# Folding a four-column projection into a padded weight tile, splitting the next weights ahead of a block's end, and joining two groups of gate matmuls

## The reference, cut to what matters

```python
def even_mixer(xn, w_in, w_out, k_ln_g, k_ln_b, rel_bias, rope_h, rope_i):
    qa, ka, va, qi, ki, wi, qb, kb, vb = _split(xn @ w_in, EVEN_SPLITS)   # qi 256, ki 64, wi 4 columns
    ...
    qi = apply_rope(qi.reshape(bsz, seq, IDX_HEADS, IDX_DIM), *rope_i)
    ki = apply_rope(layer_norm(ki, k_ln_g, k_ln_b), *rope_i)
    ya = dsa_sparse_attention(qa, ka, heads(va, A_HEADS), qi, ki, wi)
# inside dsa_sparse_attention, for each block of 128 queries:
    rel = jax.nn.relu(jnp.einsum('bqhd,bsd->bqhs', qib, k_idx))
    score = jnp.einsum('bqhs,bqh->bqs', rel, wib)
    _, idx = lax.top_k(score, topk)
def odd_mixer(xn, w_in, w_out, forget_b, sinks, rope_h):
    qc, kc, vc, fc, qd, kd, vd = _split(xn @ w_in, ODD_SPLITS)            # fc: 8 columns, the forget gate
    log_f = jax.nn.log_sigmoid(fc.astype(jnp.float32) + forget_b)
```

## Time and profile before

| | before |
|---|---|
| median of 3 runs | 1774.5 us (1773.67 to 1775.55) |
| time of the profiled execution | 1774.48 us |
| its span, first to last instruction | 1772.6 us |
| PE busy | 1748.9 us |
| DVE busy | 1075.9 us |
| ACT busy | 931.1 us |
| POOL busy | 614.6 us |
| mean granted TensorE clock | 0.998 |

### The profile page before, as it was taken

The page is one execution under the profiler, slowest core; times in us unless marked ns, Lnnn a source line. Parts: engine busy times, 40 slices in busy tenths (PEclk is TensorE's granted clock), DMA queues, the critical chain, the costliest instruction groups (busy, mean ns, idle before and its releaser), DMA issues.

```text
span 1772.6 us, 24077 instructions
## 1 busy us (share of the span) xinstructions
PE 1748.9 (99%) x8417; PEld 1417.4 (80%) x8417; DVE 1075.9 (61%) x1982; ACT 931.1 (53%) x1597; POOL 614.6 (35%) x342
## 2 busy tenths in 40 slices
PE   8999998999999999999999999999999999999998
PEld 5888777888888777778888888887778888888887
DVE  5777658999998799755455553224345655555113
ACT  6676565888886455554444443224565544444221
POOL 2333134211111322323444444444431444444442
PEclk9999999999999999999999999999999999999999
DMA  8422347999996222332233223334421333333332
GB/s 312 146 80 72 110 177 269 378 394 386 383 379 259 86 72 85 97 91 84 87 101 98 95 96 98 96 97 139 130 72 37 107 95 97 100 101 93 98 98 69
DMA packets 71623, 259.86 MB, mean 147 GB/s; under 512 B 13659, under 2 KB 18907, under 8 KB 59112
## 3 DMA queue, kind: packets, MB, share of 16 engines
q1 hardware_dynamic: 66744, 250.76, 41.4%
q0 software_dynamic: 4784, 7.85, 1.2%
HBM read 248.10 MB, written 18.43 MB: 150 GB/s over the span
## 4 chain that ended last, share of the span: by engine, by line
PE 60%; DVE 5%; issue 0%; POOL 0%; DMA 0%; SPq 0%; ACT 0%; DVEq 0%
PE ps L217 18%; PE ps L219 18%; PE ps L218 18%; DVE selb L1373 2%; DVE m L1372 1%; PE ps L571 1%; PE ps L610 1%; PE ps L599 1%; DVE prob L802 1%; DVE prob L817 1%; PE ps L585 0%; PE ps L618 0%; DVE selb L1350 0%; PE ps L633 0%; PE ps L361 0%
## 5 line engine op out<-in xcount | busy, mean ns | idle before, releaser
L284 POOL TENSOR_TENSOR ring_wl<-ring_w,ring_wh 128x1024 fp32r<-128x1024 f32 (+1 forms) x223 | 528.1, 2370 | 877.3 <-ACT ring_wh L276 771.1
L217 PE MATMUL ps<-two_x_high,ring_wh 128*128 128x512 f32 x1064 | 418.7, 394 | 1.1 <-DVE nmax L802 0.6
L218 PE MATMUL ps<-two_x_low,ring_wh 128*128 128x512 f32 x1064 | 414.2, 389 | 0.0
L219 PE MATMUL ps<-two_x_high,ring_wl 128*128 128x512 f32 x1064 | 414.2, 389 | 0.0
L276 ACT CAST ring_wh<-ring_w 128x1024 fp32r<-128x1024 f32 (+1 forms) x228 | 235.8, 1035 | 224.3 <-PE ps L219 214.8
L217 PEld LDWEIGHTS ps<-two_x_high,ring_wh 128*128 128x128 f32 x1064 | 199.7, 188 | 48.5 <-issue 4.2
L219 PEld LDWEIGHTS ps<-two_x_high,ring_wl 128*128 128x128 f32 x1064 | 199.7, 188 | 41.9
L218 PEld LDWEIGHTS ps<-two_x_low,ring_wh 128*128 128x128 f32 x1064 | 199.8, 188 | 41.8 <-issue 1.2
L1129 ACT ACTIVATE acc<-ps,param 128x512 f32<-128x512 f32 x88 | 68.6, 780 | 172.1 <-DVE ps L1149 172.1
L217 PE MATMUL ps<-hid_high,ring_wh 128*128 128x512 f32 (+1 forms) x374 | 141.0, 377 | 0.0
L218 PE MATMUL ps<-hid_low,ring_wh 128*128 128x512 f32 (+1 forms) x374 | 140.8, 377 | 0.0
(11 more groups left out here) (366 smaller groups left out, 3220.7 us busy)
## 6 DMA issues: line engine op xcount, KB each, us to landing
ring_w<-in_w_ff_up SPq DMA_DIRECT2D x88, 512.0 KB, 3.6
one_wg<-in_w_gate SPq DMA_DIRECT2D x32, 1024.0 KB, 7.8
one_wu<-in_w_up SPq DMA_DIRECT2D x32, 1024.0 KB, 8.1
one_wd<-in_w_down SPq DMA_DIRECT2D x32, 1024.0 KB, 8.6
ring_w<-in_w_ff_down SPq DMA_DIRECT2D x32, 448.0 KB, 3.3
ring_w<-in_w_da SPq DMA_DIRECT2D x23, 512.0 KB, 3.7
ring_w<-in_w_ff_down SPq DMA_DIRECT2D x16, 512.0 KB, 3.5
ring_w<-in_w_rel SPq DMA_DIRECT2D x12, 512.0 KB, 3.9
```

Source lines behind the costliest of these rows:

```text
L217: mm(out, wh, xh, start=start, stop=False)
L218: mm(out, wh, xl, start=False, stop=False)
L219: return mm(out, wl, xh, start=False, stop=stop)
L284: eng.tensor_tensor(self.low[s][:, 0:k, :], self.slab[s][:, 0:k, :], self.high[s][:, 0:k, :].bitcast(F32), ALU.subtract).then_inc(self.spl ...
```

## The change

1. The index weights `wi` take columns 64 to 67 of the key's tile in place of the key's second copy (60 columns of zeros follow). `tensor_weigh`, its weights' load (L1189), their scaling on POOL (L1261) and bank 3's four partial sums are gone. `wiT` comes from bank 0, and a plain copy takes the place of the reduction over four groups.
2. The key comes out on the lower half of the partitions only. SP copies it to the upper half by one DMA (`doubled`), issued ahead of the swaps, and PE waits for it before the key's mean.
3. `tensor_project` runs the three tiles interleaved for chunks 0 to 3, then tile by tile for chunks 4 to 7.
4. ACT rounds jobs 35 and 36 at the end of block one; DVE splits 35 and POOL 36 there. POOL's split of job 37 stays in block two.
5. In the odd layer all eight gate matmuls run in one go inside the first query's projection.

```diff
     def swap_halves(self, sp):
         raw, fin = self.buf["sraw"], self.buf["fin"]
+        sp.wait_ge(self.evac, 1)
+        sp.dma_start(raw[HD:P, 0, :], raw[0:HD, 0, :]).then_inc(self.doubled, 16)
         sp.wait_ge(self.evac, 3)
...
     def tensor_project(self, pe):
...
-        for j in range(DC):
+        order = [(i, j) for j in range(HALF) for i in range(3)] + [(i, j) for i in range(3) for j in range(HALF, DC)]
+        for i, j in order:
             pe.wait_ge(self.norms.xlow, j + 1)
...
-    def tensor_weigh(self, pe):
-        c, buf = self.c, self.buf
-        pe.wait_ge(self.w_ok, 1)
-        pe.wait_ge(self.norms.added, DC)
-        for j in range(DC):
-            at = 32 * (j % 4)
-            c.nc.tensor.matmul(c.ps[at:at + 4, 3, :], buf["ww"][:, j, :], c.h[:, j, :], start=(j < 4), stop=(j >= 4))\
-             .then_inc(self.weighed, 1)
...
     def tensor_after_q(self, pe):
         self.norms.columns(pe, 0)
-        pe.wait_ge(self.evac, 3)
+        pe.wait_ge(self.evac, 4)
+        pe.wait_ge(self.doubled, 16)
         nc.tensor.matmul(c.bank(1), c.k("blk64"), raw[:, 0, :], start=True, stop=True).then_inc(self.meaned, 1)
-        pe.wait_ge(self.evac, 4)
...
      def vector_evacuate(self, dve):
...
-            nc.vector.tensor_tensor(buf["sraw"][:, i, :], c.bank(i), rs[:, :], ALU.mult).then_inc(self.evac, 1)
-        dve.wait_ge(self.weighed, DC)
-        nc.vector.tensor_tensor(buf["wiT"][:, :], c.bank(3), rs[:, :], ALU.mult).then_inc(self.evac, 1)
+            rows = slice(0, P if i else HD)
+            nc.vector.tensor_tensor(buf["sraw"][rows, i, :], c.ps[rows, i, :], rs[rows, :], ALU.mult).then_inc(self.evac, 1)
+        nc.vector.tensor_tensor(buf["wiT"][:, :], c.bank(0), rs[:, :], ALU.mult).then_inc(self.evac, 1)
...
     block one, POOL:
-                select.gpsimd(pool)
+                ring.rest(pool, at["a0"] + 1)
     block one, ACT, after the chunks:
+                for i in range(2):
+                    ring.round(act, at["a0"] + i)
     block one, DVE, after the chunks:
+                ring.rest(dve, at["a0"])
     block two, POOL:
-                for i in (1, 2):
-                    ring.rest(pool, at["a0"] + i)
+                ring.rest(pool, at["a0"] + 2)
     block two, PE:
-                    gate.tensor(pe, 2, range(4, DC))
+                    gate.tensor(pe, 2, range(DC))
                     norms.mean(pe, 2)
-                select.tensor_weigh(pe)
...
-                gate.tensor(pe, 2, range(4))
     block two, ACT and DVE:
-                for i in range(2):
-                    ring.round(act, at["a0"] + i)
-                ring.rest(dve, at["a0"])
...
-        "w_idx": fm(np.concatenate([we[:, 1536:1792], ki, ki], axis=1)),
-        "w_idxw": mv(we[:, 1856:1860]),
+        "w_idx": fm(np.concatenate([we[:, 1536:1792], ki, we[:, 1856:1860], np.zeros((D, HD - 4), np.float32)], axis=1)),
```

More of the change, by code:

```diff
@@ L1170, with __init__ @@
 class Select:
-    def __init__(self, c, st, ring, j0, norms, buf):
-        self.c, self.ring, self.j0, self.norms, self.buf = c, ring, j0, norms, buf
-        self.w_in, self.w_ok, self.weighed = (st.sem(f"sel_{n}") for n in ("w_in", "w_ok", "weighed"))
+    def __init__(self, c, ring, j0, norms):
+        self.c, self.ring, self.j0, self.norms = c, ring, j0, norms
     def begin(self, st, buf):
-        self.buf.update(buf)
+        self.buf = buf
         (self.evac, self.meaned, self.step, self.sq, self.varred, self.rooted, self.rotated, self.ready, self.scored,
          self.reluded, self.accd, self.kready, self.logged, self.turned, self.taken, self.centred, self.wi_ok,
-         self.half, self.scaled, self.marked, self.swapped) = (
+         self.half, self.scaled, self.marked, self.swapped, self.doubled) = (
              st.sem(f"sel_{n}") for n in (
@@ L1185, in begin @@
                  "kready", "logged", "turned", "taken", "centred", "wi_ok", "half", "scaled", "marked",
-                 "swapped"))
-    def sync(self, sp):
-        sp.dma_start(self.buf["ww"][:, :, :], self.c.a["w_idxw"]).then_inc(self.w_in, 16)
+                 "swapped", "doubled"))
     def swap_halves(self, sp):
         raw, fin = self.buf["sraw"], self.buf["fin"]
+        sp.wait_ge(self.evac, 1)
+        sp.dma_start(raw[HD:P, 0, :], raw[0:HD, 0, :]).then_inc(self.doubled, 16)
         sp.wait_ge(self.evac, 3)
@@ L1198, in tensor_project @@
     def tensor_project(self, pe):
-        c, ring, x, buf = self.c, self.ring, self.norms.x, self.buf
+        c, ring, x = self.c, self.ring, self.norms.x
         w = [ring.parts(pe, self.j0 + i) for i in range(3)]
-        for j in range(DC):
+        order = [(i, j) for j in range(HALF) for i in range(3)] + [(i, j) for i in range(3) for j in range(HALF, DC)]
+        for i, j in order:
             pe.wait_ge(self.norms.xlow, j + 1)
[L1203 to L1209, removed]
-        self.norms.mean(pe, 0)
-    def tensor_weigh(self, pe):
-        c, buf = self.c, self.buf
-        pe.wait_ge(self.w_ok, 1)
-        pe.wait_ge(self.norms.added, DC)
-        for j in range(DC):
-            at = 32 * (j % 4)
-            c.nc.tensor.matmul(c.ps[at:at + 4, 3, :], buf["ww"][:, j, :], c.h[:, j, :], start=(j < 4), stop=(j >= 4))\
-             .then_inc(self.weighed, 1)
+            if j == 0:
+                pe.wait_ge(self.norms.added, i + 1)
+            mm = c.product(c.bank(i), (w[i][0][:, j, :], w[i][1][:, j, :]),
+                           (x[0][:, j, :], x[1][:, j, :]), j == 0, j == DC - 1)
+            if j == DC - 1:
+                ring.done(mm, self.j0 + i)
+        self.norms.mean(pe, 0)
     def tensor_after_q(self, pe):
@@ L1256, in tensor_free @@
         pe.wait_ge(self.reluded, 12)
[L1258 to L1262, removed]
     def scalar_square(self, act):
@@ L1300, in vector_after_q @@
         dve.wait_ge(self.turned, 1)
-        nc.vector.tensor_reduce(wi[:, :, :], c.bank(3).rearrange("p (t g e) -> p t e g", t=TT, g=4)[:, :, 0:4, :],
-                                AX_X, ALU.add).then_inc(self.wi_ok, 1)
+        nc.vector.tensor_copy(wi[:, :, :], c.bank(3).rearrange("p (t e) -> p t e", t=TT)[:, :, HD:HD + 4])\
+          .then_inc(self.wi_ok, 1)
         for i in (1, 2):
@@ L3130, in build @@
         keep = Place(nc, nc.sbuf_base)
-        mem = {"wf": {"wf": keep("wf", [P, DC, 8])}, "ww": {"ww": keep("ww", [P, DC, 4])}}
+        mem = {"wf": {"wf": keep("wf", [P, DC, 8])}}
         mem["norms"] = keep.at
@@ L3161, in build @@
             norms = Norms(c, st, Place(nc, mem["norms"], "two_"))
-            select = Select(c, st, ring, at["idx"], norms, mem["ww"])
+            select = Select(c, ring, at["idx"], norms)
             first_half(c, ring, at, mem, norms, select)
```

1 line of the change is left out of this document (removed).

## The result

The changed kernel takes 1778.96 us (median of 8 runs, 1778.09 to 1782.96); the kernel before, on the same chip, 1773.84 (8 runs, 1773.33 to 1775.55). The ratio is 1.0029, with a 95% interval of 1.0020 to 1.0038: it is slower by 5.1 us, and the forecast of 1773.7, range 1772.0 to 1777.1, was wrong in size and sign.

What follows compares the result with a forecast made beforehand. PE's matmul chain was taken to bound the kernel, with VectorE far behind. Gains of 0.46 us at the restart and 0.30 at the gate sum to 0.76 less than 1774.48: forecast 1773.7 us, range 1772.0 to 1777.1.

Steps and rivals of the forecast that it cites:

- Stall of the new order: Index projection, block one: PE waits for DVE's low parts of chunks 7 and 8, 1.19 us later from there on.
- Rounding and splitting: End of block one: job 35 at no cost; POOL's split of job 36 and drain arrive at 593.84, level with PE.
- The restart: Start of block two: PE projects at 594.86 instead of 595.32, a gain of 0.46 us.
- rival 4: PE's gap at the restart: the granted clock falls, 1.5 us lost, 1775.2; chance 0.05.
- rivals 2 and 4: Rival 2: POOL's drain is late at block one's end, all 3.3 us later than forecast, 1777.0; chance 0.12.
- The even layer's start: Rest of block two's start, costed at nothing; the key's copy lands with 1.7 us to spare.
- rival 1: Index key's last step: POOL starts before DVE on the shared ports, 0.7 us back, 1774.4; chance 0.15.
- The gate: Odd layer: eight gate chunks in one run instead of two groups, a gain of 0.30 us.
- Rival 3: Block one's end: chunks 7 and 8 aren't late, PE restarts at 593.6, 2.0 us less, 1772.5; chance 0.08.

Runs made afterwards that it cites:

- the debt paid early: Changed kernel with a small GpSimd operation and a drain ahead of POOL's split of job 36 in block one: 1773.54 us, ratio 0.9994.
- the first two experiments: Changed kernel with POOL's split of job 36 back in block two: 1775.34 us; changed kernel with small operation and drain ahead of that split: 1773.54 us.
- the order of six chunks: Changed kernel with POOL's split of job 36 in block two and the index projection interleaved for chunks 0 to 5: 1774.22 us, ratio 0.9995.

## Why the prediction was wrong

The step that failed is this one: "A drain of POOL behind a split ends at 1747.5 + 2.23 = 1749.73, 0.11 after the op's 1749.62: POOL arrives at 593.84." The operation was timed well: POOL's split ended at 18.82 us from A, against a forecast 18.69. The drain took 3.40 us behind it instead of 0.11. I had both rows before me, with 3.4 and the earlier trace rows with 0.11, and chose by the operation ahead of the drain; in these runs it depends on whether a gather or scatter has been issued since the last drain. That "the long one came soon after GpSimd's own gathers" was the right thought, used the wrong way round: in the changed kernel too the gathers were the last thing before the split, with 37.87 us idle but no drain between them. A row from the same block and queue should have weighed more than a like operation in another.

Point by point:

- *Stall of the new order*, 1.19: measured 1.28, in the changed kernel and alone. The two late products account for 1.14 of it; the product behind them takes 0.81 in place of 0.68, which the sum left out.
- *Rounding and splitting*: job 35 at no cost, as forecast; job 36 fails at the drain.
- *The restart*, 594.86 or 19.82 from A: 23.34. With the debt paid early it is 19.90.
- *The clock* (rival 4, 0.05): I held it against a gap of 1.2 us. At such a gap it stayed (1.12 and 1.17 us in the first two experiments); it fell because the gap became 4.61. I had costed rivals 2 and 4 apart, though the first makes the second likely: 1777.0 for the late meeting lacked the 2.1 us that follow from it. With 3.4 and 2.1 on top, the same sum gives 1773.7 + 5.5, that is 1779.2, against the measured 1778.96. That this comes so close is partly luck: the sum starts from 1774.48, where the kernel before has 1773.84 over 8 runs, and its gain of 0.76 was too large; with the debt paid early the odd layer's mean comes only 0.36 earlier than before. My 1.5 us for a fall was a guess at three microseconds; the slow stretch lasted some 4.5 (596.57 to about 601).
- *The even layer's start*, at nothing: right. The key's copy is hidden, by 4.1 us in the changed kernel and by 2.0 at full clock, and POOL doesn't win the race at the key's last step (rival 1) in any trace. All 23.3 us from restart to scores are unchanged at full clock (23.36 before, 23.30 and 23.37 in the first two experiments).
- *The gate*, 0.30: measured 0.34 in its place.
- *Rival 3*, that all of the gain comes: not with this order, but the order of six chunks showed it, with the 2.0 us that the prediction gave it.

## What to carry to other kernels

This was seen in one kernel; elsewhere it is something to look for. Before work is put between a queue's last gather or scatter and the end of a block, look at how long that queue's drain took behind its last operation: if the drain was long but idle, it can stand behind the new work and move everyone's meeting. Drain early, while the engine waits anyway, or leave the work on the far side. And price a longer gap of TensorE together with the clock behind it: the two rivals that I priced apart were one case.

## What was unexpected of the hardware

- GpSimd's first drain behind gathers and scatters ended 3.4 to 3.5 us after its last operation (4.2 and 2.7 with drains in between), the next one about 0.1 after. In the changed kernel it didn't matter that GpSimd had been idle for 37.87 us in between, the last 31.6 of them after its last gather had landed. What the time goes to is not visible in the trace.
- The granted clock stayed at 1.00 over TensorE gaps of 0.47, 1.12, 1.17, 1.19 and 1.85 us at this place, and fell over one of 4.61; the four steps behind it took 1.44, 1.28, 1.28 and 0.93 us, 2.1 us in all more than at full clock, and the next 0.70.
